# Attention stage: two 128-row products per score tile, and probabilities scaled by their inverse sums before they are turned

## The reference

```python
s = jnp.einsum('bqhr,bqkr->bhqk', ql, c_sel).astype(jnp.float32) * (HEAD_DIM ** -0.5)
s = s - slopes[None, :, None, None] * dist[:, None]
s = jnp.where((idx <= t_pos[None, :, None])[:, None], s, -jnp.inf)
p = jax.nn.softmax(s, axis=-1)
return jnp.einsum('bhqk,bqkr->bqhr', p.astype(c_sel.dtype), c_sel)
```

## Time and profile before

| what | us |
|---|---|
| median of 3 runs | 3894.07 (3891.0 to 3894.65) |
| the profiled execution | 3891.9 |
| its span in the profile | 3890.1 |
| TensorE, VectorE, ScalarE, GpSimd busy in the span | 3525.0, 1913.2, 1094.5, 560.7 |
| the attention stage | about 2577 to 3020 |

### The profile page before, as it was taken

One profiled execution on the slowest core, in us unless ns is written; L12 is line 12 of the kernel. 1 busy time (PEld: TensorE's weight loads), 2 busy tenths in 40 slices (PEclk: granted clock), 3 DMA queues, 4 the chain that ended last, 5 costly groups with the idle time before them and its releaser, 6 DMA issues. The chain is left out here.

```text
span 3890.1 us, 39586 instructions
## 1 busy us (share of the span) xinstructions
PE 3525.0 (91%) x15200; PEld 2739.0 (70%) x15200; DVE 1913.2 (49%) x2838; ACT 1094.5 (28%) x1710; POOL 560.7 (14%) x393
## 2 busy tenths in 40 slices
PE   7999788889788898999999998888889889999998
PEld 5776567657577586888888767755455768888886
DVE  4325444567441434555544549679666332424244
ACT  3222333233331222221112441134455221111112
POOL 0003364620100001100001200000045210000000
PEclk8999899889899999999999999988899989999999
DMA  3132332310231013322222202022111311111111
GB/s 115 71 101 83 112 116 76 119 62 1 95 87 60 12 49 108 109 92 97 93 86 76 76 11 60 30 58 54 41 25 28 119 38 44 54 43 54 43 54 54
DMA packets 221268, 263.18 MB, mean 68 GB/s; under 512 B 16827, under 2 KB 149844, under 8 KB 219074
## 3 DMA queue, kind: packets, MB, share of 16 engines
q1 hardware_dynamic: 221124, 261.22, 21.2%
HBM read 218.89 MB, written 29.18 MB: 64 GB/s over the span
## 5 line engine op out<-in xcount | busy, mean ns | idle before, releaser
L192 PE MATMUL psum<-rounded,rounded 128*128 128x512 f32 (+2 forms) x3936 | 1547.5, 393 | 181.3 <-POOL rounded L935 35.7
L193 PE MATMUL psum<-rounded,rounded 128*128 128x512 f32 (+2 forms) x3936 | 1537.3, 391 | 0.0
L194 PE MATMUL psum<-rounded,rounded 128*128 128x512 f32 (+2 forms) x3936 | 1536.3, 390 | 0.0
L192 PEld LDWEIGHTS psum<-rounded,rounded 128*128 128x128 f32 x3936 | 752.2, 191 | 359.3 <-POOL rounded L935 37.8
L194 PEld LDWEIGHTS psum<-rounded,rounded 128*128 128x128 f32 x3936 | 750.9, 191 | 153.2
L193 PEld LDWEIGHTS psum<-rounded,rounded 128*128 128x128 f32 x3936 | 752.1, 191 | 149.7 <-issue 0.2
L2714 DVE TENSOR_TENSOR plain<-psum,plain 128x512 f32<-128x512 f32 x432 | 288.6, 688 | 111.8 <-PE psum L194 110.1
L2725 DVE TENSOR_TENSOR plain<-psum,plain 128x512 f32<-128x512 f32 x44 | 30.4, 692 | 438.5 <-ACT plain L2634 438.5
L3091 DVE TENSOR_SCALAR_CACHE_REDUCE plain<-plain,plain 128x384 bf16<-128x384 f32 (+2 forms) x204 | 181.9, 942 | 1.3
L2706 DVE TENSOR_TENSOR rounded<-plain,rounded 128x512 fp32r<-128x512 f32 x108 | 96.4, 892 | 173.8 <-ACT rounded L2623 173.7
L3230 PE MATMUL psum<-plain,plain 128*128 128x512 f32 (+3 forms) x384 | 168.3, 551 | 0.9 <-ACT plain L3346 0.9
(11 more groups left out here) (299 smaller groups left out, 3595.0 us busy)
## 6 DMA issues: line engine op xcount, KB each, us to landing
plain<-in_ff_w_dram SPq DMA_DIRECT2D x64, 512.0 KB, 5.5
plain<-in_w_ada_dram SPq DMA_DIRECT2D x96, 256.0 KB, 3.3
plain<-in_w_gu_dram SPq DMA_DIRECT2D x44, 512.0 KB, 4.9
plain<-in_w_in_dram SPq DMA_DIRECT2D x36, 512.0 KB, 3.8
plain<-in_c_fwd_dram SPq DMA_DIRECT2D x64, 256.0 KB, 2.6
rounded<-rounded SPq DMA_DIRECT2D x48, 256.0 KB, 3.3
plain<-in_w_down_dram SPq DMA_DIRECT2D x22, 512.0 KB, 3.6
fold<-plain SPq DMA_DIRECT2D x8, 1024.0 KB, 4.7
```

The lines of the kernel that those rows point to most:

```text
L192: nc.tensor.matmul(out, wh, xh, start=first, stop=False)
L193: nc.tensor.matmul(out, wh, xl, start=False, stop=False)
L194: return nc.tensor.matmul(out, wl, xh, start=False, stop=last)
```

## The change

It does six things:

- Scores: both products have 128 rows. The low part of q is laid out twice in the SBUF set (`l0`, `l1`), against k high and k low; `mixt.hi` no longer holds it. A set has six tiles in place of four, and `copies` issues nine DMAs in place of six.
- Probabilities: `exponent` also accumulates its row sum. VectorE then takes the reciprocal of that 128 x 1 sum and multiplies the probabilities in place (`scaled(n)`), and `turns(n)` waits for this, not for `exponent(n)`. In VectorE's list `scaled(n)` stands after `biased(n + 1)`.
- Values: no columns of ones (the GpSimd memsets go), and no `divided`. ScalarE's `high(m)` rounds the product from PSUM for each block, and VectorE's `low(m)` subtracts.
- `sparse_values` and the GpSimd step that waits for it come one loop earlier.
- The load of `w_uv` moves from `phase_latent` to the start of SP's list in `phase_attention`, ahead of the first bias.
- The gate row: the attention stage loads only 512 of its columns, after step 112's scores; the next stage loads the whole row first on SP, and GpSimd waits for it.

```diff
@@ Stacks
-        q0, q1, k0, k1 = (part.bitcast(F32) for part in self.sets[p % 2])
+        q0, q1, l0, l1, k0, k1 = (part.bitcast(F32) for part in self.sets[p % 2])
...
+        sp.wait_ge(S["pair_lo"].sem, S["pair_lo"].at(2 * p + 1))
+        sp.dma_start(l1[64:P, :], l0[64:P, :]).then_inc(S["odd_copied"].sem, 16)
+        sp.dma_start(l1[0:64, :], l0[64:P, :]).then_inc(S["odd_copied"].sem, 16)
...
         sp.dma_start(q0[64:P, :], q0[0:64, :]).then_inc(S["even_copied"].sem, 16)
+        sp.dma_start(l0[64:P, :], l0[0:64, :]).then_inc(S["even_copied"].sem, 16)
...
-            last = nc.tensor.matmul(out, low[rows, tile], k[rows, a:b], start=False, stop=True)
+            last = nc.tensor.matmul(out, low[:, tile], k[:, a:b], start=False, stop=True)
@@ phase_latent, SP and GpSimd
-            sp.dma_start(wuv, ap["w_uv_2"][0].rearrange("h r d -> r h d")).then_inc(S["wuv_loaded"].sem, 16)
-                nc.gpsimd.memset(value_columns(va, t)[:, :, 64:128], 1.0)
@@ phase_attention, SP
+            sp.dma_start(wuv.rearrange("p (h d) -> p h d", d=HD), ap["w_uv_2"][0].rearrange("h r d -> r h d")).then_inc(S["wuv_loaded"].sem, 16)
             bias(0)
...
-                    sp.dma_start(gate, core.modulations[:, 2 * D:3 * D].partition_broadcast(P)).then_inc(S["gate_loaded"].sem, 16)
...
+            sp.dma_start(gate, core.modulations[:, 2 * D:2 * D + BANK].partition_broadcast(P)).then_inc(S["gate_loaded"].sem, 16)
@@ TensorE
-                pe.wait_ge(S["act_done"].sem, S["act_done"].at(n + 1))
+                pe.wait_ge(S["row_ready"].sem, S["row_ready"].at(n + 1))
@@ VectorE
-            def divided(m):
...
-                nc.vector.reciprocal(inverse[rows, :], ps[sums, 6 + m % 2, :]).then_inc(S["dve_chain"].sem, 1)
...
-                nc.vector.tensor_tensor(mixt.raw[rows, h // 2, b * BANK:(b + 1) * BANK], ps[rows, 6 + m % 2, :], inverse[rows, :], ALU.mult).then_inc(S["row_ready"].sem, 1)
+            def scaled(n):
+                h, i = steps[n]
+                w, one = (i + 1) * P, slice(n % 16, n % 16 + 1)
+                dve.wait_ge(S["act_done"].sem, S["act_done"].at(n + 1))
+                nc.vector.reciprocal(total[:, one], total[:, one]).then_inc(S["dve_chain"].sem, 1)
+                dve.wait_ge(S["dve_chain"].sem, S["dve_chain"].at(n + 1))
+                nc.vector.tensor_scalar(probs[n % 2][:, 0:w], probs[n % 2][:, 0:w], total[:, one], None, ALU.mult).then_inc(S["row_ready"].sem, 1)
...
+                nc.vector.tensor_tensor(mixt.lo[rows, h // 2, cols], ps[rows, 6 + m % 2, :], mixt.hi_raw[rows, h // 2, cols], ALU.subtract).then_inc(S["ft_lo"].sem, 1)
...
             for n in range(N + 5):
                 if n + 1 < N:
                     biased(n + 1)
...
+                    scaled(n)
                 if n in finished_at:
+                    low(finished_at[n])
@@ ScalarE
+                nc.scalar.activation(probs[n % 2][:, 0:w], probs[n % 2][:, 0:w], ACT.Exp, scale=-1.0, bias=least[:, one], accum_out=total[:, one]).then_inc(S["act_done"].sem, 1)
...
+                nc.scalar.activation(mixt.hi[rows, h // 2, cols], ps[rows, 6 + m % 2, :], ACT.Copy).then_inc(S["ft_hi"].sem, 1)
```

More of the change, by code:

```diff
@@ L1909, in _ @@
         def _(sp):
+            if modulated is not None:
+                sp.dma_start(gate, core.modulations[:, 2 * D:3 * D].partition_broadcast(P)).then_inc(S["gate_loaded"].sem, 16)
             for p in range(4):
@@ L2840, in __init__ @@
         self.core, self.mixt = core, mixt
-        self.sets = [[core.view_r(6 + 16 * s + 4 * k, 1, L)[:, 0, :] for k in range(4)] for s in range(2)]
+        self.sets = [[core.view_r(6 + 24 * s + 4 * k, 1, L)[:, 0, :] for k in range(6)] for s in range(2)]
     def high(self, act, p, k):
@@ L2878, in scores @@
         if i == 0 and e == 0:
-            pe.wait_ge(S["even_copied"].sem, S["even_copied"].at(32 * (p + 1)))
-        rows, tile = slice(64 * e, 64 * e + 64), slice(i * P, (i + 1) * P)
-        q, k, low = self.sets[p % 2][e], self.sets[p % 2][2 + e], self.mixt.hi[:, p, :]
-        w = (i + 1) * P
+            pe.wait_ge(S["even_copied"].sem, S["even_copied"].at(48 * (p + 1)))
+        q, low, k = (self.sets[p % 2][2 * part + e] for part in range(3))
+        w, tile = (i + 1) * P, slice(i * P, (i + 1) * P)
         for a in range(0, w, BANK):
@@ L2913, in _ @@
             sp.dma_start(grow, ap["kv_norm_g_2"][0].partition_broadcast(P)).then_inc(S["loaded1"].sem, 16)
-            sp.dma_start(wuv, ap["w_uv_2"][0].rearrange("h r d -> r h d")).then_inc(S["wuv_loaded"].sem, 16)
             stacks.copies(sp, 0)
-        @block.gpsimd
-        def _(pool):
-            for t in range(TT):
-                nc.gpsimd.memset(value_columns(va, t)[:, :, 64:128], 1.0)
         @block.scalar
@@ L3159, in phase_attention @@
     biases = [core.view(186 + 4 * s, L) for s in range(2)]
[L3160 to L3164 removed]
+    turned = [core.view3(150, 4, BANK), core.view3(54, 8, BANK)]
+    narrow, wide = [core.view(202, 448), core.view(158, BANK)], [core.view(198, L), core.view(CKVT_KB, L)]
+    masked = lambda n: (narrow if n < FIRST + 4 else wide)[n % 2]
+    mdist, gate = core.view(203.75, L), core.view(158, BANK)
+    least, total = core.tiny2[:, 0:16], core.tiny2[:, 16:32]
     HEADS, DENSE = 16, 8
@@ L3170, in phase_attention @@
     pair = lambda n, w: ps[:, 2 * (n % 2):2 * (n % 2) + 2, :].rearrange("p a b -> p (a b)")[:, 0:w]
-    finished_at = {e + (4 if m == 2 * DENSE - 1 else 5): m for m, e in enumerate(ends)}
+    finished_at = {e + (3 if m == 2 * DENSE - 1 else 5): m for m, e in enumerate(ends)}
     with nc.Block() as block:
@@ L3252, in _ @@
                 for m in range(blocks):
-                    if 1 <= n - ends[m] <= 4:
+                    if 1 <= n - ends[m] <= 4 and not (m == 2 * DENSE - 1 and n == FIRST + 3):
                         values(m, n - ends[m] - 1)
-                if n == FIRST + 3:
+                if n == FIRST + 2:
+                    values(2 * DENSE - 1, 3)
                     sparse_values()
@@ L3273, in _ @@
                 pool.wait_ge(signal.sem, signal.at(16))
-                wide = gate[:, 0:BANK].unsqueeze(1).to_broadcast([P, KT // 2, BANK])
-                nc.gpsimd.tensor_tensor(raw, raw, wide, ALU.mult).then_inc(S["w2_scaled"].sem, 1)
+                rows = gate.unsqueeze(1).to_broadcast([P, KT // 2, BANK])
+                nc.gpsimd.tensor_tensor(raw, raw, rows, ALU.mult).then_inc(S["w2_scaled"].sem, 1)
         @block.vector
@@ L3312, in _, with low @@
+            def low(m):
+                h, b = m // 2, m % 2
+                rows, cols = slice(64 * (h % 2), 64 * (h % 2) + 64), slice(b * BANK, (b + 1) * BANK)
+                dve.wait_ge(S["ft_hi"].sem, S["ft_hi"].at(m + 1))
+                nc.vector.tensor_tensor(mixt.lo[rows, h // 2, cols], ps[rows, 6 + m % 2, :], mixt.hi_raw[rows, h // 2, cols], ALU.subtract).then_inc(S["ft_lo"].sem, 1)
             biased(0)
-            for n in range(N + 6):
+            for n in range(N + 5):
                 if n + 1 < N:
@@ L3319, in _ @@
                         stacks.low(dve, h // 2 + 1, i - 4)
-                if n - 2 in finished_at and finished_at[n - 2] // 2 % 2 == 1:
-                    low(finished_at[n - 2])
+                    scaled(n)
                 if n in finished_at:
-                    divided(finished_at[n])
-                if n == N + 5:
-                    low(blocks - 1)
+                    low(finished_at[n])
                 if n < CHOSEN_BY:
@@ L3380, in _ @@
                         slopes(h + 1)
-                if n == FIRST + 4:
+                if n in finished_at:
+                    high(finished_at[n])
+                if n == FIRST + 2:
                     sparse_values()
-                if n - 1 in finished_at and finished_at[n - 1] // 2 % 2 == 1:
-                    high(finished_at[n - 1])
-    for n in ("mm_done", "tr_done", "dve_done", "act_done", "probs_turned"):
+    for n in ("mm_done", "tr_done", "dve_done", "act_done", "probs_turned", "row_ready", "dve_chain"):
         S[n].close(N)
-    for n in ("aux_done", "row_ready", "dve_chain"):
+    for n in ("aux_done", "ft_hi", "ft_lo"):
         S[n].close(blocks)
-    for n in ("ft_hi", "ft_lo"):
-        S[n].close(HEADS)
     for n in ("aux2_done", "act_free", "x_ready"):
@@ L3428, in second_block @@
     stacks = Stacks(core, mixt)
-    phase_latent(core, stacks, va, beside=lambda dve: selection.rounds(dve, 8.0))
+    phase_latent(core, stacks, beside=lambda dve: selection.rounds(dve, 8.0))
     w_out = ap["w_out_2"].rearrange("a (k p) n -> p (a k) n", p=P)
```

67 lines of the change are left out of this document (23 added, 44 removed).

## The result

| | before | after |
|---|---|---|
| median, us (4 runs each) | 3894.11 (3891.0 to 3894.65) | 3974.99 (3969.61 to 3977.74) |
| ratio after / before | | 1.0208 [1.019, 1.0225] |
| span of the profiled execution, us | 3890.1 | 3974.9 |
| TensorE, VectorE, ScalarE, GpSimd busy, us | 3525.0, 1913.2, 1094.5, 560.7 | 3486.3, 1940.4, 1122.3, 558.1 |

The kernel is 80.9 us slower by the medians and 84.8 us by the profiled spans. VectorE's busy time rose by 27 us only and TensorE's fell by 39, so the rest is waiting. The windows of the kernel after: the eight dense heads, six sparse heads, and head 7 by itself, a dense head with neither selection work nor the split of a next pair beside it. The columns are those of the earlier trace rows.

The account below looks back on a forecast made before the run. TensorE, 91% busy, leads before; then the serial TensorE-VectorE ring bounds attention. Dense +30, sparse +102, sparse values -3, tail -4, `w_uv` +1: +126 on 3891.9 gives 4018, median 2 higher, so 4020 us; range 3925 to 4080.

Parts of the forecast that it names:

- A: Main case, whole program: serial loop plus GpSimd delaying the sparse multiply, 4020 us, own range 3970 to 4075; chance 0.58.
- the ring: Attention loop: transposes, scores, biased tile, reciprocal and multiply in series between TensorE and VectorE, 23.9 us a head.
- The dense heads: First eight attention heads: 248.8 us against 218.5, +30, from the ring plus split, selection and clock.
- clock: TensorE's granted clock in the attention heads: 0.84 assumed, a third of the time at half speed, 2.5 us a head.
- selection: Selection pieces on VectorE in dense heads 0 to 6: 4 us a head added, between 1.6 and 7.
- split: VectorE's `stacks.low` ahead of the multiply: 1.22 us eight times in eight dense heads, 1.2 us a head.
- The sparse heads: Last eight attention heads: GpSimd's bias instruction delays the multiply 1.22 us a step; 37.1 us against 24.3, +102.
- rival B: Sparse heads: multiply not held up by GpSimd, 27.3 us a head, program 3942 us; chance 0.17.
- Sparse values, tail, `w_uv`, gate: Remaining attention terms: shorter wait -3 us, shorter stage end -4, earlier `w_uv` load +1, gate load hidden.
- C: Faster: no clock or selection cost in the dense heads (25.1 us each), no GpSimd hold-up; 3874 us, chance 0.10.
- D: Score products do not get faster, 64 rows not causing the 0.40 us pitch: +43, 4063 us; chance 0.09.
- E: Multiply by its column runs as slowly as a biased tile, 0.753 us for 0.52: +30, 4050 us; chance 0.06.

## Why the prediction was right, and where its sizes were off

Forecast 4020 (3925 to 4080), slower; measured 3975.0, slower and inside the range. The case that came true is A, with its mechanism: the lead is gone, the ring sets the end, and GpSimd holds up the multiply. The forecast of +126 against +85 is off by 41 us. It would be off by 49 without the 7.9 us that stand ahead of the latent stage and are not the change's: that much of the nearness is luck.

- **The ring, right.** The transposes wait for the multiply and the biased tile for the scores. Forecast 23.9 us a head at full clock, measured 22.6 in head 7. The 1.3 us lie mostly in the small reciprocal: the estimates put 0.31 us between the end of the biased tile and the multiply, and the timeline has 2795.19 - 2795.07 = 0.12, which is 1.5 us a head. The first product behind transposes takes 0.31 and not 0.23, which goes the other way by 0.6.
- **The dense heads, wrong: forecast +30, measured -7.2.** This is the step that failed. The additions on top of the ring were mis-sized: 57.6 us forecast over the stretch (clock 20, selection 28, split 9.6) against 30.5 measured (selection 14.6, split 15.9). The selection costs 2.1 a head and not 4. The split went the other way, 4.0 in the four heads with it, 2.3 in the mean of heads 0 to 6, against 1.2. With these, 22.6 + 2.3 + 2.1 = 27.0, which is what the seven heads took in the mean, so nothing is left over for the clock as a term on top (forecast 2.5 a head). What the clock takes is inside the two measured terms, and how much that is was not shown; it was granted at 0.90 where I took 0.84. The ring was 10 us too long. I took the clock from the old kernel's dense heads on the reasoning that a TensorE which idles more gets no more clock. Busy fell from 87 to 69% and the grant rose from 0.84 to 0.90. In the sparse heads busy fell from 90 to 63% and the grant fell from 0.96 to 0.80, so these rows give no rule in either direction.
- **The sparse heads, right in cause and near in size.** Forecast 37.1 a head, measured 35.6. The multiply is held up by 1.19 us a step (forecast 1.22), and ends 0.08 to 0.55 us after GpSimd, by its width (forecast 0.3 to 0.4). Two errors cancel in the rest: without the hold-up a head takes 24.1 and not the 27.3 of rival B, while the hold-up is worth 11.5 with its clock, and not 9.8. The Trainium skill, "SBUF — State Buffer", section "Who interferes with whom", says that a `tensor_scalar` in a two-port mode and an instruction of GpSimd exclude each other, and that the one which issues first holds the ports. The traces agree: 1713 ns against 520 in the mean where GpSimd comes first, and a longer GpSimd instruction beside a multiply of its own length where the multiply starts 0.22 us or more ahead. It also excepts the form with an accumulator, and the trace agrees with that (1279 ns at 1024 columns with GpSimd beside it, never held up).
- **Sparse values, tail, `w_uv`, gate.** Forecast -3 and -4. Heads 8 and 15 got 7.5 and 7.9 us longer; less a sparse head's 11.3 each, that is -3.8 and -3.4, near the forecast. From the start of the latent stage to the first biased tile 1.3 us were added (forecast 1). The gate's load stayed hidden (-0.5 in the next stage).
- **The rivals.** B fell: the multiply got in first in one of 48 steps. Its condition was made true by one wait and gave 3893.5, not 3942, since its other terms were the same mis-sized ones. C's sign for the dense heads was right (26.4 a head, below its point of 27.3, though above its own 25.1), and it was wrong about the whole, for the hold-up that it left out. D fell: the pitch is 0.23. The Trainium skill, "TensorEngine Tiling (Array Packing)", section "Key Properties", says that a change of tiling mode drains the array; the pitch of 0.23 against 0.41 agrees with it, though no record shows the drain itself. D's price was also too low: it put +43 on products that do not get faster, and the kernel with 64-row products took 113 more. E fell: the mean of 517 ns is the forecast's 520.

## What to carry to other kernels

When an operation is put in series between two engines that take turns, draw the ring and look at what each of them has in its list ahead of the thing the other one wants; here the place of one call, and then the choice of ScalarE for it, turned +81 us into -52 against the kernel before. Two engines in each other's way show in a profile as an instruction whose time does not follow its width and whose end follows another engine's, and one wait added to that other engine can be cheaper than the contention (here worth 81 us). Take the clock and the slack of an old bound with care when the bound moves: measure the least disturbed unit (here a head at full clock), and add the parts one by one.

## What the runs showed that I had not expected

- The order in which two records start does not tell which of them waits. In the sparse step shown, the multiply's record begins 0.04 us before GpSimd's (3081.19, 3081.23), and the multiply is the one that waits. Without the reciprocal it begins 0.23 us before (2845.80, 2846.03), and GpSimd is the one that waits. The one step of the kernel after in which GpSimd starts 0.32 us behind the multiply goes the same way. Some 0.2 us of a 128 x 1 instruction decides over most of 87 us.
- An instruction form that is 70% slower in itself (1279 ns against 753) makes the kernel 57 us faster, 48 from the first biased tile on, because nothing holds it up.
- Another VectorE instruction can hold up GpSimd. Where the split of a next pair, a subtraction of two SBUF tiles, starts 0.2 us ahead of GpSimd's 1024 columns in the kernel after, these take 3.19 us in place of 2.34, and the multiply behind the split is held up in its turn (2.44 us).
- A 64-row product between 128-row ones costs 0.18 to 0.20 us more for each product of the pair at 512 columns (0.41 to 0.43 against 0.23), and 0.10 for the first one behind transposes (0.41 against 0.31). That is 64 us here when TensorE leads, and 113 to 114 with the ring on VectorE, with a granted clock of 0.62 to 0.78. The cause of that low clock stays open.
- The stages ahead of the attention, which all edits but that of the selection leave alone, vary by up to 10.8 us from one profiled execution to another (first biased tile at 2579.0 to 2589.8). That is as much as the totals of one kernel vary over more runs (12 us over 13 runs of the kernel before), so a difference of 10 us between single executions says little unless it is placed in a stage.
